# A hybrid decoder step: ScalarE's side work moved between split and eviction, GpSimd's multiplies moved to other engines, the final state moved behind a chunk

## What is computed

```
z, xbc, dt_raw, u, v, ga, gb = split_cols(h @ W['w_in'][l], IN_SIZES)
ya, hs, cs = ssd_branch(z, xbc, dt_raw, conv0[l], ssm0[l], ...)   # causal conv, silu, chunked scan, gate, norm
yb, vr = chunk_mlp_branch(jax.nn.gelu(u), jax.nn.gelu(v), ...)    # layernorm of v, spatial product in chunks of 128
merged = jax.nn.sigmoid(ga) * (ya @ W['w_ssd_out'][l]) + jax.nn.sigmoid(gb) * (yb @ W['w_cmlp_out'][l])
x = x + g1 * rmsnorm(merged @ W['w_o'][l], W['mix_post_g'][l])
```

```
mix = cb[..., None] * decay * dtc[:, None]
y_in = jnp.einsum('btsgr,bsgrp->btgrp', mix, xc)
y_st = jnp.einsum('btgn,bgrpn->btgrp', cc, h) * jnp.exp(cum)[..., None]
h_new = h * jnp.exp(last)[..., None, None] + jnp.einsum('bsgn,bsgr,bsgrp->bgrpn', bc, w_end, xc)
```

## Time and profile before

| | |
|---|---|
| median of three runs | 1922.27 us (1920.86 to 1924.54) |
| the profiled execution | 1918.96 us, span of its trace 1917.1 us |
| TensorE busy | 1758.5 us, 92% of the span |
| VectorE, ScalarE, GpSimd busy | 1340.9, 1038.0, 116.6 us |
| chain that ended last | TensorE 81%, VectorE 9%, ScalarE 5% |
| mixer of layer 0, of layer 1 | about 84 to 440 us, 696 to 1012 us |

### The profile page before, as it was taken

One profiled execution on the slowest core, in us unless ns is written; L12 is line 12 of the kernel. 1 busy time (PEld: TensorE's weight loads), 2 busy tenths in 40 slices (PEclk: granted clock), 3 DMA queues, 4 the chain that ended last, 5 costly groups with the idle time before them and its releaser, 6 DMA issues.

```text
span 1917.1 us, 33371 instructions
## 1 busy us (share of the span) xinstructions
PE 1758.5 (92%) x13192; PEld 1636.8 (85%) x13192; DVE 1340.9 (70%) x1318; ACT 1038.0 (54%) x1063; POOL 116.6 (6%) x128
## 2 busy tenths in 40 slices
PE   6998999869999969989796999999999999999994
PEld 4887898768999869889795999989898989899993
DVE  3765456754444488765756788878887888788884
ACT  2445545323333334664342776767676777677771
POOL 4022101000000002310100000000000000000000
PEclk8999998989999979999896999999999999999996
DMA  9987542337886436662240999999999999999980
GB/s 274 293 264 256 174 155 89 121 123 228 278 286 213 144 99 188 209 193 95 88 147 18 340 352 345 350 301 351 347 350 312 334 351 347 335 318 352 344 314 23
DMA packets 379498, 465.09 MB, mean 243 GB/s; under 512 B 10404, under 2 KB 351604, under 8 KB 379379
## 3 DMA queue, kind: packets, MB, share of 16 engines
q1 hardware_dynamic: 372370, 441.65, 70.4%
q0 software_dynamic: 6720, 20.86, 3.4%
q10 hardware_dynamic: 304, 1.08, 0.2%
HBM read 452.84 MB, written 10.92 MB: 242 GB/s over the span
## 4 chain that ended last, share of the span: by engine, by line
PE 81%; DVE 9%; ACT 5%; issue 3%; DMA 2%; POOL 0%; DVEq 0%; SPq 0%; ACTq 0%; POOLq 0%
PE psum L404 10%; PE psum L415 10%; PE psum L409 9%; PE psum L1204 9%; PE psum L1209 9%; PE psum L1206 9%; PE psum L1228 4%; PE psum L1232 4%; PE psum L1229 4%; PE psum L444 2%; PE psum L762 2%; ACT whi L343 1%; DVE wlo L348 1%; PE psum L1163 1%; PE psum L1180 1%
## 5 line engine op out<-in xcount | busy, mean ns | idle before, releaser
L370 DVE TENSOR_TENSOR wlo<-raw,whi 128x2048 fp32r<-128x2048 f32 x219 | 501.6, 2292 | 107.8 <-ACT whi L365 107.0
L348 DVE TENSOR_TENSOR wlo<-raw,whi 128x2048 fp32r<-128x2048 f32 x113 | 264.8, 2344 | 266.3 <-ACT whi L343 266.0
L365 ACT ACTIVATE whi<-raw 128x2048 fp32r<-128x2048 f32 x219 | 418.4, 1912 | 31.6 <-PE psum L1232 30.0
L404 PE MATMUL psum<-xhi,whi 128*128 128x264 f32 x1584 | 243.7, 310 | 51.4 <-ACT xhi L1292 40.5
L404 PEld LDWEIGHTS psum<-xhi,whi 128*128 128x128 f32 x1584 | 220.5, 206 | 72.3 <-issue 59.4
L343 ACT ACTIVATE whi<-raw 128x2048 fp32r<-128x2048 f32 x113 | 216.6, 1917 | 92.9 <-PE psum L415 72.4
L409 PE MATMUL psum<-xlo,whi 128*128 128x264 f32 x1584 | 214.4, 289 | 0.0
L415 PE MATMUL psum<-xhi,wlo 128*128 128x264 f32 x1584 | 214.3, 289 | 0.0
L409 PEld LDWEIGHTS psum<-xlo,whi 128*128 128x128 f32 x1584 | 206.1, 195 | 0.0
L1204 PE MATMUL psum<-whi,hghi 128*128 128x256 f32 x1408 | 202.2, 286 | 3.1 <-issue 2.2
L415 PEld LDWEIGHTS psum<-xhi,wlo 128*128 128x128 f32 x1584 | 201.2, 191 | 0.0
(11 more groups left out here) (360 smaller groups left out, 1939.9 us busy)
## 6 DMA issues: line engine op xcount, KB each, us to landing
raw<-in_exp_wd_dram SPq DMA_DIRECT2D x76, 1024.0 KB, 5.0
raw<-in_exp_wg_dram SPq DMA_DIRECT2D x72, 1024.0 KB, 6.6
raw<-in_exp_wu_dram SPq DMA_DIRECT2D x72, 1024.0 KB, 6.7
raw<-in_w_in_dram SPq DMA_DIRECT2D x52, 1024.0 KB, 5.3
raw<-in_w_mod_dram SPq DMA_DIRECT2D x17, 1024.0 KB, 5.3
hf<-in_exp_wu_dram SPq DMA_DIRECT2D x16, 1024.0 KB, 6.2
hf<-in_exp_wg_dram SPq DMA_DIRECT2D x16, 1024.0 KB, 6.4
hf<-in_exp_wd_dram SPq DMA_DIRECT2D x12, 1024.0 KB, 5.0
```

Of the source, the lines that this page charges most:

```text
L348: dve.tensor_tensor(wlo[slot], raw[slot], whi[slot].bitcast(F32), ALU.subtract) \
L365: act.activation(whi[j % R3], raw6[slot], ACT.Copy).then_inc(sem["hi_ready"], 1)
L370: dve.tensor_tensor(wlo[j % R3], raw6[slot], whi[j % R3].bitcast(F32), ALU.subtract) \
L404: pe.matmul(out, whi[slot][:, k, j * P:(j + 1) * P], hi(k), start=first and k == 0, stop=False)
```

## The change

- `act_phase` loses `after`; all of ScalarE's side work goes into `ahead`, between the split of the next chunk and the eviction of this one. Steps that followed the eviction of chunk c now mostly stand with chunk c+1.
- The decay of a sample's state moves from GpSimd to ScalarE: `scale(b)`, eight scaled copies in place, behind `outer(b)`. `outer_ready` counts twice per sample.
- Samples: 0 at z's last chunk, 1, 2, 3 at chunks 0, 2, 3 of v, 4 and 5 at chunks 1 and 2 of u, 6 and 7 at chunks 0 and 1 of ga. VectorE takes each one chunk later or in the same chunk, TensorE's rows go with them.
- The Silu of the last five convolution tiles moves behind the last eviction of z. The turn of the samples' B and C goes one chunk earlier on TensorE.
- Half of v's gain and bias goes to VectorE.
- `tokens(0)` and `segments(0)` go one chunk earlier on VectorE, `keep_b(0)` in front of the eviction on ScalarE.
- ce times C goes from GpSimd to VectorE, inside `masked(1)`, which moves in front of a split.
- The final state is finished behind the split of the normalised y; its turn stands behind ssd_out's first chunk, its copy at the second.
- GpSimd fetches states 0 and 1 before 2. The output copy at the start signals a semaphore of its own, `conv_keep`.

```diff
@@ act_phase
-        def act_phase(act, key, count, epilogue=None, peel=0, end=False, after=None, ahead=None):
+        def act_phase(act, key, count, epilogue=None, peel=0, end=False, ahead=None):
...
-                    if after:
-                        after(c + 2 * i)
@@ GpSimd
-                def decay(b):
-                    pool.wait_ge(s_in[b % SR3], 16 * (l * PER[b % SR3] + b // SR3 + 1))
-                    pool.tensor_tensor(sring[b % SR3], sring[b % SR3], bc(spx[:, :, b], 2, [P, KT, NS]), ALU.mult) \
-                        .then_inc(sem["samp_decayed"], 1)
-                pool.wait_ge(sem["w_turned"], l + 1)
-                fetch_state(2)
                 pool.wait_ge(sem["tail_out"], 32 * (l + 1))
                 fetch_state(0)
                 fetch_state(1)
+                pool.wait_ge(sem["w_turned"], l + 1)
+                fetch_state(2)
...
                         fetch_state(b + 2)
-                        decay(b + 2)
@@ ScalarE
+                def scale(b):
+                    act.wait_ge(s_in[b % SR3], 16 * (l * PER[b % SR3] + b // SR3 + 1))
+                    for k in range(KT):
+                        ins = act.activation(sring[b % SR3][:, k, :], sring[b % SR3][:, k, :], ACT.Copy,
+                                             scale=spx[:, k, b:b + 1])
+                    ins.then_inc(sem["outer_ready"], 1)
...
+                def sample(b):
+                    outer(b)
+                    scale(b)
...
-                gates("z", zs, ACT.Silu, after_z)
+                gates("z", zs, ACT.Silu, ahead=ahead_z)
+                act.wait_ge(sem["conv_part"], 9 * l + 9)
+                act.activation(xcv[:, 7:CT, 0:S], xcv[:, 7:CT, 0:S], ACT.Silu)
@@ VectorE, masked
+                        if c:
+                            dve.wait_ge(sem["ce_exp"], 2 * (l + 1) - g)
+                            ins = dve.tensor_tensor(ce[:, g * R:(g + 1) * R, :], ce[:, g * R:(g + 1) * R, :],
+                                                    bc(xcv[:, KT + G + g, Q:2 * Q], 1, [P, R, Q]), ALU.mult)
...
+                masked(1)
                 split_lo(dve, n + 3, 0)
-                masked(1)
@@ VectorE, ga
+                        dve.wait_ge(sem["v_root"], l + 1)
+                        for t in range(HT):
+                            ins = dve.tensor_scalar(vb[:, t, :], vb[:, t, :], row("cmlp_ln_g", l, t),
+                                                    row("cmlp_ln_b", l, t), ALU.mult, ALU.add)
+                        ins.then_inc(sem["v_normed"], 1)
```

More of the change, by code:

```diff
@@ L32 @@
 ys_hi ys_ready scattered scat_added moe_done
-route_arg y_normed merged y_turned y_copied y_out dve_chain""".split()
+route_arg y_normed merged y_turned y_copied y_out conv_keep dve_chain""".split()
 def hybrid_ssd_chunkmlp_moe_step(nc, A, O):
@@ L489, in body @@
                         epilogue(i, c, acc[:, 2 * pair:2 * pair + 2, 0:T]).then_inc(acc_free[pair], 1)
-                    if after:
-                        after(c + 2 * i)
-            loop(act, count // 2, body, count // 2 if end or after or n0 <= MB else peel)
+            loop(act, count // 2, body, count // 2 if end or ahead or n0 <= MB else peel)
         def dve_phase(dve, key, count, epilogue=None, peel=0, cols=T, end=False, after=None):
@@ L1020, in after_gb @@
                         spread_cum(0)
-                for name, after in (("xbc", after_xbc), ("z", after_z), ("v", lambda c: sample_rows(c + 1)), ("u", after_u),
+                for name, after in (("xbc", after_xbc), ("z", after_z), ("v", after_v), ("u", after_u),
                                     ("ga", after_ga), ("gb", after_gb)):
@@ L1050, in _, with after_ssd @@
                         .then_inc(sem["gate_ssq"], 1)
[L1052 to L1057, removed]
+                def after_ssd(c):
+                    if c == 0:
+                        pe.wait_ge(sem["st_ready"], (l + 1) * NQ)
+                        for k in range(KT):
+                            ins = pe.transpose(ms[:, 2 + k // 4, (k % 4) * P:(k % 4 + 1) * P], hT[:, k * P:(k + 1) * P],
+                                               ident[:, :])
+                        ins.then_inc(sem["st_turned"], 1)
+                pe_phase(pe, ("ssd_out", l), KT // MT, xs(xhi), xs(xlo), T, ready=5 * l + 3, after=after_ssd)
                 def add_squares(c):
@@ L1371, in after_z, with ahead_v, ahead_u, ahead_ga @@
                         act.activation(bct[0:B, :], ms[0:B, 2, :], ACT.Copy).then_inc(sem["bc_ready"], 1)
+                        act.wait_ge(sem["conv_part"], 9 * l + 5)
+                        act.activation(xcv[:, 0:7, 0:S], xcv[:, 0:7, 0:S], ACT.Silu)
                     if c == 3:
-                        act.wait_ge(sem["conv_part"], 9 * l + 9)
-                        act.activation(xcv[:, 7:CT, 0:S], xcv[:, 7:CT, 0:S], ACT.Silu)
-                        outer(0)
-                def after_v(c):
-                    outer(c + 1)
-                def after_u(c):
-                    if c == 1:
-                        act.wait_ge(sem["v_centered"], l + 1)
-                        act.activation(hf[:, :, :], vb[:, :, :], ACT.Square).then_inc(sem["v_sq"], 1)
-                        outer(5)
-                def after_ga(c):
-                    if c == 0:
+                        sample(0)
+                def ahead_v(c):
+                    if c == 0:
+                        sample(1)
+                    if c >= 2:
+                        sample(c)
+                def ahead_u(c):
+                    if c == 1 or c == 2:
+                        if c == 2:
+                            act.wait_ge(sem["v_centered"], l + 1)
+                            act.activation(hf[:, :, :], vb[:, :, :], ACT.Square).then_inc(sem["v_sq"], 1)
+                        sample(3 + c)
+                def ahead_ga(c):
+                    if c == 0:
+                        sample(6)
+                    if c == 1:
                         act.wait_ge(sem["v_root"], l + 1)
-                        for t in range(KT):
+                        for t in range(HT, KT):
                             ins = act.activation(vb[:, t, :], vb[:, t, :], ACT.Identity, bias=row("cmlp_ln_b", l, t),
@@ L1870, in after_v @@
                 def after_v(c):
-                    sample(c)
+                    if c < 2:
+                        sample(c)
+                    if c == 3:
+                        sample(2)
                 def after_u(c):
                     if c == 0:
-                        sample(4)
+                        sample(3)
                     if c == 1:
@@ L1881, in after_u @@
                     if c == 2:
-                        sample(5)
+                        sample(4)
                     if c == 3:
@@ L1885, in after_u @@
                         mean_inv(rs[:, 0, :], ms[:, 2, 0:T], D, sem["v_inv"])
+                        sample(5)
                 def after_ga(c):
```

112 lines of the change are left out of this document (55 added, 57 removed).

## The result

The changed kernel takes 1877.62 us in the median (1874.37 to 1882.67, four runs), the kernel before beside it 1922.74: a ratio of 0.977 (95% interval 0.974 to 0.979). The prediction said 1880. The profiled execution of after took 1876.30 (span 1874.5), that of before 1918.96: 42.7 us less.

What follows compares the result with a forecast made beforehand. It took TensorE to bound the kernel: its own work, its waits and the lower clock. Gains of 22.3 us in layer 0 and 16.0 in layer 1, together 38.3 off 1918.96, gave 1880.7, forecast as 1880; range 1869 to 1897.

Steps and rivals of the forecast that it cites:

- Side work behind the split: Between z and v, ScalarE splits the next weights first, so TensorE's wait goes: 8.84 us in layer 0, 6.2 in layer 1.
- mod rows: In layer 0, ScalarE copies them right behind the split, so TensorE's five waits for them go: 4.4 us.
- Decay on ScalarE: In the sample chunks, eight scaled copies per sample take 2.15 us on ScalarE, hidden behind TensorE's work; no gain counted.
- So it is hidden: Between z and v's first chunks, the tightest pair: ScalarE's split ends at 12.1 us, TensorE wants it at 12.5.
- ga: In ga, TensorE's waits shrink to 1.2 and 1.0 us: gain 3.3 in layer 0 and 4.0 in layer 1.
- Tokens and segments earlier: In gb, b is copied before the eviction: the 1.02 us gap goes and the spread shortens, 2.0 a layer.
- the spread becomes like the second one, 3.83: The first spread of the running sums falls from 4.80 to 3.83 us of work, a gain of 0.97.
- ce and the state: Behind the second chunk's segments, TensorE starts on y earlier and the reciprocal comes 4.8 us earlier: 3.8 a layer.
- ScalarE as the bound: Rival: scaled copies cost what the normalisation does, 1.95 us more per sample in v and ga: 1893, chance 0.11.
- waited for a state: Rival: a scaled copy waits in ScalarE's queue for a state's arrival, delaying eviction and split: slower, 1928 at 15.5, chance 0.04.
- the sum: All terms over both layers' mixers: 22.3 us in layer 0 and 16.0 in layer 1, together 38.3.

Runs made afterwards that it cites:

- the held kernel: The kernel before with one line added: GpSimd holds its first three decays until VectorE has finished the convolution; 1905.57 us, ratio to before 0.992.

## Why the prediction was right, point by point

- **Side work behind the split** (15.0 predicted in both layers, mod rows 4.4): the size was about right and the mechanism was half of it. The reading of the earlier trace rows, "The split needs none of this; it only stands behind it in the queue", is true but stops short: it takes the Silu's wait of 4.44 as given. That wait was GpSimd's doing, and the held kernel gets 12 to 20 us without a change of order. The order does the same and more: in layer 1, with GpSimd beside VectorE, only 1.42 reaches TensorE. Of the excess of 3.0 in layer 0 half is a slow pass in xbc that the profiled before had and after had not (3.64 in place of 2.22). That half is chance: when the same kernel ran again, the pass took 3.72 and 3.74 in the two layers, and against that execution the stage gained 14.7 and 4.9. The other half belongs to the six waits: each cost some 0.25 more than its idle time, which the prediction left out (from sample rows to sample rows 9.03 us around the wait of 0.46 in the earlier trace rows, 8.32 without a wait in after).
- **Decay on ScalarE**: "So it is hidden" held between z and u. The copies took 2.48 for eight and not 2.15: the term was mis-sized by 0.33 a sample, inside its bounds. The Trainium skill, page "ScalarE: Activation LUTs", section "Rules for kernel authors", makes it an estimate of 3.25; the trace has 2.48, nearer the row. The prediction credits the move with no gain of its own, and it has none: with the decay on GpSimd the time is the same, and the waits that are left in ga are gone.
- **ga**: waits of 1.2 and 1.0 predicted, 0.92 and 0.68 measured, without a slow pass behind them (granted clock 1.00). The gain was 4.6 and 6.0 for 3.3 and 4.0; the prediction had left out the slow second pass of before and a wait of 0.46 in layer 1.
- **Tokens and segments earlier**: 2.0 predicted, 1.1 measured. The step that failed is "the spread becomes like the second one, 3.83": the gap went, but in the profiled execution the spread took 4.48 and 4.80 and the pass behind it 3.89. When the same kernel ran again the spread took 3.83 in both layers, so its length differs between executions of one kernel. What the edit is shown to bring is the 1.0 of the gap, the prediction's lower bound.
- **ce and the state**: TensorE's start and the reciprocal came as worked out (5.5 for 5.57 and 5.0 earlier for 4.8). The gain was 3.2 and 3.4 for 3.8. Of the 5.0, the transposes take back 0.8, as forecast, and what the sum lacked is the lo pass behind the wait for y (L409): before, the transposes broke that wait into 1.41 and 3.63, and the pass took 2.18 and 2.21 (granted clock 0.95 in layer 0); now TensorE idles 4.73 in one piece, and it takes 3.09 and 2.93 (0.63 and 0.67).
- **The rivals**: ScalarE as the bound is the nearest: 1.8 us more per sample already cost 9.6. No scaled copy waited for a state: a fetch lands in 6.7 us in the median after, 7.6 in the earlier trace rows.
- **The total**: the traces show 42.1 us for the 38.3 of the sum, made of errors of both signs (3.3 too little for the first stage and 3.3 for ga, 1.9 too much for the spread and 1.0 for the state). That the forecast lies within 3 us of the median is in part luck.

## What to carry to other kernels

When a queue waits for another engine, read that engine's durations too, against the same instruction elsewhere in the trace: a pass that takes three times its usual time (4.59 for 1.53 here) may point to a neighbour, and holding the neighbour back for a few us can be one line. On an engine that feeds the next stage and also does side work, put what the next stage needs first; where a piece of side work runs matters far less once it stands behind that. Parts of a change that share one chain don't add: undo them one at a time before giving each its share.

## What the runs showed of the hardware

- VectorE and GpSimd slow each other: three GpSimd multiplies, 1.91 each alone, took 7.49 beside VectorE's convolution, whose passes lost 4.6 (layer 0 of before); a split took 4.00 in place of 2.29, two masked products 4.52 in place of 2.44. The Trainium skill, page "SBUF — State Buffer", section "Who interferes with whom", says that a VectorE instruction with two SBUF inputs contends with a GpSimd instruction that reads SBUF. The traces agree, and by the run that held GpSimd back in the kernel before, the price was 12 to 20 us here.
- The stretch between the two spreads of the running sums in a layer took 32.3 us in both layers of after, and 29.2 and 30.7 when the same kernel ran again (the spread alone 4.80 and 3.83 in layer 1). The passes behind the first spread of layer 1, by the windows of after and then of the second run (columns as in the earlier trace rows):

```profile
853.00:859.30 6.30, 6.30 (x34) 6.08 (x34) 5.11 (x11) 4.39 (x12) 0.00 (x0) 0.61 0.00 0
```

```profile
850.40:856.00 5.60, 5.60 (x35) 5.54 (x34) 5.10 (x11) 4.50 (x13) 0.00 (x0) 0.70 0.00 0
```

  TensorE is busy throughout and the clock is partly at 1.2 GHz, behind 32 products of only 16 rows (4.80 us in after). How long it stays there differs between runs of the same code: a granted clock of 0.61 and 0.70. The smaller spread in xbc does the same: the pass behind it in layer 0 took 3.64 us at a granted clock of 0.55 in before, 2.22 at 1.00 in after, and 3.72 when after ran again. So 1.5 to 3 us a layer between two profiles are no evidence for an edit; what decides it wasn't settled.
- A small copy on ScalarE from SBUF costs 0.22 us at 128 columns without a pointer operand and 0.31 with one, in rows of eight (1.75 and 2.48).
